# Forget bias of the samples by way of DRAM and VectorE instead of TensorE, with its transfers ahead of the output projection's weights

## What is computed

```
ft   = cumsum(concat(cache_logf[page_table], logf))         # per sample and head, 264 steps
sc   = einsum(q, k_all) * scale
bias = ft[:, :, past:, None] - ft[:, :, None, :]
p    = softmax(where(mask, sc + bias, -inf))                # the ft of the query drops out
y    = einsum(p, v_all)
```

## Time and profile before

| | us |
|---|---|
| median of 3 runs (1370.23 to 1373.33) | 1373.27 |
| the profiled execution | 1372.02 |
| its span, first to last instruction | 1370.3 |
| TensorE busy in the span | 1304.2 (95%) |
| VectorE busy | 357.1 (26%) |
| ScalarE busy | 207.7 (15%) |
| mean rate of the DMA queues | 358 GB/s |

### The profile page before, as it was taken

The page is one execution under the profiler, slowest core; times in us unless marked ns, Lnnn a source line. Parts: engine busy times, 40 slices in busy tenths (PEclk is TensorE's granted clock), DMA queues, the critical chain, the costliest instruction groups (busy, mean ns, idle before and its releaser), DMA issues.

```text
span 1370.3 us, 15525 instructions
## 1 busy us (share of the span) xinstructions
PE 1304.2 (95%) x6186; PEld 580.5 (42%) x6186; DVE 357.1 (26%) x754; ACT 207.7 (15%) x475; POOL 38.4 (3%) x79
## 2 busy tenths in 40 slices
PE   5999999999999999999999999999999999999896
PEld 2656466655463433434344342334334343343332
DVE  2542225766452121112122111211211122121122
ACT  2124424411221100101011010101101010010101
POOL 1100002000020000000000000000000000000000
PEclk9999999999989999999999999999999999999998
DMA  9836586789676999999999999999999999999993
GB/s 345 285 141 266 185 281 173 208 230 260 233 281 242 414 428 428 428 428 427 427 426 428 428 427 428 401 426 425 428 428 429 428 422 429 428 427 428 427 427 137
DMA packets 71905, 491.06 MB, mean 358 GB/s; under 512 B 11814, under 2 KB 24862, under 8 KB 44053
## 3 DMA queue, kind: packets, MB, share of 16 engines
q1 hardware_dynamic: 68564, 480.86, 86.9%
q0 software_dynamic: 3264, 9.13, 2.5%
HBM read 484.77 MB, written 5.18 MB: 358 GB/s over the span
## 4 chain that ended last, share of the span: by engine, by line
PE 65%; DMA 30%; DVE 2%; issue 1%; SPq 1%; ACT 0%; DVEq 0%
PE bank L1949 29%; DMA ring<-in_w_gate_up_dram 27%; PE bank L1632 8%; PE bank L1658 4%; PE bank L1937 3%; PE bank L2016 2%; PE bank L1620 2%; PE bank L1506 2%; PE bank L1787 2%; PE bank L1913 2%; DMA ring<-in_w_in_dram 1%; PE bank L1572 1%; PE bank L1914 1%; PE bank L2044 1%; PE bank L1940 1%
## 5 line engine op out<-in xcount | busy, mean ns | idle before, releaser
L1949 PE MATMUL bank<-ring,work 128*64 128x512 f32 x1984 | 439.9, 597 | 11.2 <-issue 5.9
L1949 PEld LDWEIGHTS bank<-ring,work 128*64 128x64 f32 x1984 | 155.2, 137 | 281.7 <-issue 281.7
L1949 PE MATMUL bank<-ring,hT 128*64 128x512 f32 x896 | 206.2, 608 | 14.1 <-DMA ring<-in_w_gate_up_dram 14.1
L1449 DVE TENSOR_TENSOR gbT<-gbT,bank 128x512 f32<-128x512 f32 x80 | 55.0, 688 | 436.6 <-PE bank L1940 301.6
L1949 PEld LDWEIGHTS bank<-ring,hT 128*64 128x64 f32 x896 | 69.1, 139 | 148.6 <-issue 148.6
L1632 PE MATMUL bank<-hT,ring 128*128 128x320 f32 x384 | 106.8, 439 | 2.1 <-DMA ring<-in_w_in_dram 2.1
L1405 DVE TENSOR_SCALAR work<-bank 128x512 f32<-128x512 f32 x32 | 22.0, 687 | 317.9 <-PE bank L1949 299.1
L1632 PEld LDWEIGHTS bank<-hT,ring 128*128 128x128 f32 x384 | 73.3, 192 | 36.3 <-issue 5.9
L1658 PE MATMUL bank<-hT,ring 128*128 128x320 f32 x256 | 73.6, 437 | 0.2 <-ACT gaT L705 0.2
L1937 PE MATMUL bank<-work 128*128 128x512 f32 x128 | 67.8, 631 | 0.0
L842 ACT ACTIVATE work<-bank 128x320 f32<-128x320 f32 x15 | 6.6, 438 | 394.0 <-PE bank L1506 394.0
(11 more groups left out here) (375 smaller groups left out, 913.0 us busy)
## 6 DMA issues: line engine op xcount, KB each, us to landing
ring<-in_w_gate_up_dram SPq DMA_DIRECT2D x128, 2048.0 KB, 16.0
ring<-in_w_down_dram SPq DMA_DIRECT2D x64, 2048.0 KB, 17.3
ring<-in_w_ada_dram SPq DMA_DIRECT2D x12, 2048.0 KB, 10.6
ring<-in_w_in_dram SPq DMA_DIRECT2D x12, 2048.0 KB, 11.0
ring<-in_cache_k_dram SPq DMA_DIRECT2D x64, 128.0 KB, 6.6
ring<-in_cache_v_dram SPq DMA_DIRECT2D x16, 512.0 KB, 6.4
ring<-in_w_out_dram SPq DMA_DIRECT2D x2, 2048.0 KB, 12.7
out_dram<-tok POOLq DMA_DIRECT2D x2, 1024.0 KB, 8.5
```

Of the source, the lines that this page charges most:

```text
L1449: TTo(piece(gbf, i), piece(gbf, i), B[6 + n % 2][:, :], ALU.add).then_inc(s["scatter_read"], 1)
L1949: last = mm(bank[CAP * x:CAP * x + CAP, :], lhsT[:, CAP * x:CAP * x + CAP], rhs(x), start=start, stop=stop)
```

## The change

The bias leaves TensorE. `cached_logf` becomes two full transposes and one small matmul, for which the cached pages are stored in another order and the new log forget values are spread by sample (`lfnew`). VectorE makes `Fs`, now one row for each sample and head, at the start of prompt pair 7, ahead of `keys_turned(0)`. SP then writes it to DRAM with 16 DMAs, waits until they have landed, and reads it back with 9 DMAs that repeat each row for the 8 queries: the bias of sample b lies in `qT[:, b, 0:256]` (the prompt's queries are done with by then), that of the new columns in `Ftail`. These stand ahead of `chunk(23)`. `sample_max(b)` adds the bias where it copied before, `sscores(b)` has two matmuls fewer.

```diff
+        sbias_d = nc.dram_tensor("sample_bias", (DB, 4, 4, PAST), f32, kind="Internal").ap()
+        stail_d = nc.dram_tensor("sample_tail", (4, 4, DB, DS), f32, kind="Internal").ap()
...
             values_in(0)
             values_in(1)
+            eng.wait_ge(s["F_made"], 2)
+            for b in range(DB):
+                rows = Fs[H * b:H * b + H, :]
+                eng.dma_start(sbias_d[b].rearrange("u g n -> g u n"), rows[:, 0:PAST]).then_inc(s["bias_out"], 16)
+                eng.dma_start(stail_d[:, :, b, :].rearrange("u g q -> g u q"), rows[:, PAST:PAST + DS]).then_inc(s["bias_out"], 16)
+            eng.wait_ge(s["bias_out"], 16 + 32 * DB)
+            eng.wait_ge(s["scores_ps"], H)
+            for b in range(DB):
+                eng.dma_start(qT[:, b, 0:PAST], sbias_d[b].rearrange("u g n -> (u g) n").unsqueeze(1).to_broadcast([H, DS, PAST])).then_inc(s["bias_in"], 16)
+            eng.dma_start(Ftail, stail_d.rearrange("u g b q -> (u g) (b q)").unsqueeze(1).to_broadcast([H, DS, NS])).then_inc(s["bias_in"], 16)
             chunk(23)
             chunk(25)
             keys_in(2)
...
-                V_.tensor_copy(P[:, 0:PAST], ps[:, 0:PAST]).then_inc(s["sscores_read"], 1)
+                if b == 0:
+                    eng.wait_ge(s["bias_in"], 96 + 16 + 16 * DB)
+                TTo(P[:, 0:PAST], ps[:, 0:PAST], qT[:, b, 0:PAST], ALU.add).then_inc(s["sscores_read"], 1)
...
+                new = P[:, PAST + DS * b:PAST + DS * b + DS]
+                link(TTo(new, new, Ftail[:, DS * b:DS * b + DS], ALU.add))
...
                 if p == NT - 1:
+                    eng.wait_ge(s["tr_ps"], G_CF + 1)
+                    link.later(TS(Fs[:, 0:PAST], B[1][:, 0:PAST], -1.0, None, ALU.mult))
+                    link(TS(Fs[:, PAST:PAST + DS], B[0][:, 0:DS], -1.0, None, ALU.mult))
+                    link(V_.tensor_copy(r1, ones[:, 0:2]))
+                    V_.tensor_tensor_scan(Fs, onesf, Fs, 0.0, ALU.mult, ALU.add).then_inc(s["F_made"], 1)
...
-            eng.wait_ge(s["tr_ps"], G_CF + 1)
-            link.later(V_.tensor_copy(Fs[:, :, 0:PAST], B[1][:, :].rearrange("p (s c) -> p s c", s=2)))
...
-            for n in range(2):
-                link(V_.tensor_tensor_scan(Fs[:, n, :], onesf, Fs[:, n, :], 0.0, ALU.mult, ALU.add))
-            TS(Fs, Fs, -1.0, None, ALU.mult).then_inc(s["F_made"], 1)
...
-                for g in range(4):
-                    q = 32 * g
-                    for n in range(2):
-                        for i in range(NPG):
...
+                eng.wait_ge(s["sample_consts"], 1)
+                for i in range(NPG):
+                    tr(B[1][:, 128 * i:128 * i + 128], lfc[:, DB * i:DB * i + DB, :].rearrange("p b h -> p (b h)"), 128)
+                mm(B[0][:, 0:DS], lfnew, at_token, start=True, stop=True).then_inc(s["tr_ps"], 1)
...
-                mm(ps[:, 0:PAST], hsel[q:q + H, :], Fs[q:q + H, n, 0:PAST], start=False, stop=False)
-                mm(ps[:, PAST + DS * b:PAST + DS * b + DS], hsel[q:q + H, :], Fs[q:q + H, n, PAST:PAST + DS], start=False, stop=True)\
-                    .then_inc(s["sscores_ps"], 1)
...
             values(NT - 1)
-            eng.wait_ge(s["F_made"], 2)
```

More of the change, by code:

```diff
@@ L933, in _ @@
             link(V_.reduce_sum(hm4, groups.rearrange("p g h q -> p h g q"), AX.XY))
+            own = ident[0:NS, 0:NS].rearrange("p (b q) -> p b q", q=DS)
+            link.later(V_.reduce_sum(in_sample, own, AX.X))
+            link(V_.reduce_sum(at_token, own.rearrange("p b q -> p q b"), AX.X))
             eng.wait_ge(s["rows_ps"], 1)
@@ L1171, in _ @@
                     head_max(2 * p + 5)
-            eng.wait_ge(s["tr_ps"], G_CF + 1)
-            link.later(V_.tensor_copy(Fs[:, :, 0:PAST], B[1][:, :].rearrange("p (s c) -> p s c", s=2)))
-            for g in range(4):
-                q = 32 * g
-                ins = V_.tensor_copy(Fs[q:q + 32, :, PAST:PAST + DS], B[0][q:q + 32, 0:NS].rearrange("p (s c) -> p s c", s=2)[:, :, DS * g:DS * g + DS])
-                link.later(ins)
-            link(V_.tensor_copy(r1, ones[:, 0:2]))
-            for n in range(2):
-                link(V_.tensor_tensor_scan(Fs[:, n, :], onesf, Fs[:, n, :], 0.0, ALU.mult, ALU.add))
-            TS(Fs, Fs, -1.0, None, ALU.mult).then_inc(s["F_made"], 1)
             queries(0)
@@ L1699, in cached_logf @@
                 eng.wait_ge(s["scores_read"], H - 2)
-                for g in range(4):
-                    q = 32 * g
-                    for n in range(2):
-                        for i in range(NPG):
-                            page_ = NPG * (4 * n + g) + i
-                            mm(B[1][q:q + 32, PAST * n + 128 * i:PAST * n + 128 * i + 128], lfcf[:, H * page_:H * page_ + 32], ident[:, :],
-                               start=True, stop=True)
-                    last = mm(B[0][q:q + 32, 0:NS], lftf[0:NS, 2 * H:2 * H + 32], ident[0:NS, 0:NS], start=True, stop=True)
-                last.then_inc(s["tr_ps"], 1)
+                eng.wait_ge(s["sample_consts"], 1)
+                for i in range(NPG):
+                    tr(B[1][:, 128 * i:128 * i + 128], lfc[:, DB * i:DB * i + DB, :].rearrange("p b h -> p (b h)"), 128)
+                mm(B[0][:, 0:DS], lfnew, at_token, start=True, stop=True).then_inc(s["tr_ps"], 1)
             scores(0)
@@ L1737, in sscores @@
                         t = 2 * g + odd
-                        mm(ps[32 * g:32 * g + 32, 0:PAST + NS], Qbd[:, b % 2, t, :], KT[:, b % 2, t, :],
-                           start=(odd == 0), stop=False)
-                mm(ps[:, 0:PAST], hsel[q:q + H, :], Fs[q:q + H, n, 0:PAST], start=False, stop=False)
-                mm(ps[:, PAST + DS * b:PAST + DS * b + DS], hsel[q:q + H, :], Fs[q:q + H, n, PAST:PAST + DS], start=False, stop=True)\
-                    .then_inc(s["sscores_ps"], 1)
+                        last = mm(ps[32 * g:32 * g + 32, 0:PAST + NS], Qbd[:, b % 2, t, :], KT[:, b % 2, t, :],
+                                  start=(odd == 0), stop=(odd == 1))
+                last.then_inc(s["sscores_ps"], 1)
             def sweights(b):
```

29 lines of the change are left out of this document (14 added, 15 removed).

## The result

| | before | changed |
|---|---|---|
| median, us | 1373.27 (1369.76 to 1373.73, 5 runs) | 1380.06 (1377.83 to 1382.48, 5 runs) |
| profiled execution, us | 1372.02 | 1382.41 |
| its span, us | 1370.3 | 1380.7 |
| last `svalues`, us from the start | 373.83 | 387.15 |
| TensorE busy, us | 1304.2 | 1297.6 |

The ratio is 1.0059, with a 95% interval of 1.0044 to 1.0075. The same kernel, timed a second time beside the experiments, gave 1.0061 (1.0044 to 1.0078). The forecast was 1377.5 in a range of 1370.5 to 1384.0.

What follows compares the result with a forecast made beforehand. The DMA queue, through the landing of sample 2's keys, was taken to set the samples' start: 8.0 us later keys, 0.2 chain, less 4.5 on TensorE, plus 1.5 clock, +5.2 on 1372.3 gives 1377.5 us, range 1370.5 to 1384.

Steps and rivals of the forecast that it cites:

- The bound and the mechanism: Ahead of `svalues(0)`: sample 2's keys land 8.0 us later, outweighing 4.5 us saved on TensorE in six samples.
- The write trip: On SP: `Fs` ready at 272.1, 16 writes 6.7 us, landing 2.3 us, first read at 281.1.
- the mark of 285: Start of SP's reads: before 278 or after 285 would correct the price of the writes.
- From the first read to the keys: DMA queue to sample 2's keys: 16.7 us as before, plus bias 3.3, plus `chunk(23)` 5.5, less 0.5 overlap.
- The overlap with GpSimd's read: GpSimd's prompt read falls partly ahead of the bias, easing the keys' path by 0.5 us; 3.4 at most.
- The chunk's own landing: `chunk(23)` lands at about 295, `gate_job("gb", 4)` ends near 300, ahead of `svalues(0)`: no cost of its own.
- The clock: TensorE's idle time ahead of `svalues(0)` lowers its clock: 1.5 us taken, between nothing and 2.5 us.
- one sign: Profile after: from `svalues(0)` to the first `w_gate_up` DMA, 4.5 us less than before.
- The sum: Whole kernel: 8.0 keys, 0.2 longer chain, less 4.5 TensorE, plus 1.5 clock: +5.2 us on 1372.3.
- (C): Not slower, transfers hidden: 1362 to 1368; decided by sample 2's keys landing less than 4.3 us later; chance 0.05 plus 0.02.
- (A): Sample 2's keys are late by more than what is saved: +4 to +11, 1376 to 1383; chance 0.57.
- (D): Slow trip: 0.6 us a write, 5.2 for landing, bias at the cached keys' rate: 1383 to 1389; chance 0.06.

Runs made afterwards that it cites:

- the fillers: Changed kernel with 14, then 8, independent matmuls in TensorE's wait ahead of `svalues(0)`: 1379.94 us (ratio 1.0053) and 1381.48 us (1.0078).
- both moves: Changed kernel with `chunk(23)` issued ahead of the DRAM trip and two writes instead of sixteen: 1367.99 us, ratio 0.9975.
- all three steps: Changed kernel with `chunk(23)` first, two writes, six bias reads behind sample 2's keys, GpSimd's prompt read behind sample 3's scores: 1368.80 us, ratio 0.9981.

## Why the prediction came out right

**The bound and the mechanism** held; of the sizes, several were off, and that the total lies in the range is in part luck (below). What sets the samples' start is the landing of sample 2's keys, as read from the wait of 4.60 us in the earlier trace rows, and it is more than TensorE's saving. From their landing to `svalues(0)` it is 4.8 us (4.6 forecast). The six later sample scores are 0.75 us shorter each, and no new wait of note stands in samples 1 to 7. The landing itself was forecast 8.0 us late and came 12.9 us late.

**The write trip** was sized too low. `Fs` was ready at 271.3 (272.1 forecast). But a write took 0.65 us (10.4 us for 16) and not 0.42. The size in bytes doesn't set it: the 32-byte rows took as long as the 1 KB rows, and the plain write of 128 rows of 1 KB, with eight times the bytes, 0.33. And the landing took 4.9 us and not 2.3. The prediction took the 2.3 because "it is the same queue"; what counted was what another queue was doing, GpSimd's read, which had been seen, but was given only 0.5 us and to the other side. The first read went out 5.5 us later than forecast (286.6, not 281.1), just past the mark of 285 which the prediction had set for that.

**From the first read to the keys**: forecast 25.0 us, measured 24.4, but by terms that were off against each other. The bias took the 6.4 us that SyncE needs to issue 9 reads and the chunk behind them, not 3.3 by bytes (each read lands 2.5 us after its issue, and the DMA share from 286.6 to 292.4 us is 0.49, so bytes were not the limit). The overlap with GpSimd's read gave 3.4 us, the bound, and not 0.5 (16.7 us from `chunk(25)` to the keys before, 13.3 with the gate chunk ahead of the trip). The chunk was 4.7 to 5.3 us in place of 5.5. The chunk's own landing cost nothing, as said: TensorE waited 2.73 us for it inside a longer wait, though it came at 300.75 and not at about 295, and `gate_job("gb", 4)` ended at 307 and not near 300.

**The clock** cost 4.7 us in one profile and 2.1 in the other, where 1.5 was taken and 2.5 was the bound. It is why one sign failed: from `svalues(0)` to the first `w_gate_up` DMA there should be 4.5 us less than before, and it is 62.97 us against 62.74.

**The sum.** In the profile `svalues(7)` is 13.3 us late where the terms gave 8.0 + 0.2 - 4.5 + 1.5 = 5.2. Measured, they are 12.9 for the landing, 0.2 for the chain behind it, -4.5 for TensorE and 4.7 for the clock. So the prediction was saved in part by what it didn't count, and that is luck. 2.9 of the 13.3 us come back behind the samples: the low clock at the router doesn't occur in the profile after, its 16 matmuls taking 1.97 us (from the last `svalues` to the first expert 38.9 us against 40.6), and the experts take 954.7 us against 955.9. And the profiled execution was 2.4 us above the median, that of before 1.3 below. What is left is 6.8 us between the medians, against +5.2 from a base set 1 us lower. Whether the router's clock is low differs from profile to profile without regard to the change, as said at the fillers. From the last `svalues` to the end the profiles of these kernels range from 991 to 997 us; what sets this spread was not tried.

**A slip without weight.** Against (C) the prediction says that 7.6 MB in 17 us is more than the 380 GB/s that the queue reaches; the earlier trace rows shows 414. The 7.6 MB would need 447, so the argument holds.

**The rivals.** (A), forecast with 0.57, came true as 1376 to 1383, with 1380.06. Of (D), its 0.6 us a write and its landing of 5.2 came nearly true (0.65 and 4.9), but not its price, since the bias didn't run at the keys' rate and GpSimd's read was out of the way. (C), not slower, is what the kernel becomes once the landing is no more than 4.3 us late, as the prediction put its turning point: with both moves the keys land 28.7 us behind the start of the prompt's last softmax product (268.68 to 297.38), against 28.0 before (270.11 to 298.14), so 0.7 us later, and the kernel is 0.25% faster.

## What to carry to other kernels

When results go through DRAM inside a queue that also prefetches, count the issues of each write and read, and look for what stands behind them: a prefetch that doesn't need the trip belongs ahead of its wait. Make the layout on the chip so that the trip takes two DMAs and not sixteen. Look at what the other queues move while the trip waits for its landing. And moving one landing forward helps only until the next one is late: here the first two moves were worth 12.7 us at the keys, and up to 7.7 us more at the same place changed nothing in the time that could be measured, since the cached values then came late.

## What the runs showed of the hardware

The time a small write needs to be confirmed depends on other queues: 1.1 to 1.2 us from the end of its issue with idle DMA engines, 4.3 to 5.0 us in five profiles in which a read of 1.3 MB on GpSimd's queue filled them. For 3.4 us of that read nothing of SyncE's queue started. The Trainium skill, DMA: Bandwidth & Descriptors, section Queues, rings and completion order, says that each engine takes turns between its queues and drains a whole packet of typically 9 to 17 descriptors before it switches. The larger part of the read, `x_prompt`, is 256 rows of 4 KB, 16 for each of the 16 engines if they are spread evenly (an estimate), which is one such packet; so a wait for most of the read doesn't speak against the rule. The trace records single rows; how they were grouped for the engines no run here shows.

A DMA issue on SyncE took 0.58 us with a gap of 0.04 for most of the writes of 16 permuted rows, of 32 bytes and of 1 KB alike, about the same for a repeating read of 128 KB (5.07 us for 8) and for a 2 MB chunk right behind them; 0.33 us for a plain write of 128 rows of 1 KB, 0.73 for the one of 128 rows of 32 bytes behind it. The shape isn't all: the same 2 MB chunk took 0.39 to 0.43 us where it was issued by itself.

The low clock after a wait cost the same program 2.1 us in one execution and 4.7 in another, over the first sample. The Trainium skill, TensorE: Matmul & The Clock Gate, section Part 1: The HAM clock gate, has an idle stretch bring the throttled clock back; the windows at 0.50 to 0.53 behind the waits of 6.61 and 8.84 us agree, and with a wait of only 1.15 us ahead of `svalues(0)`, in the kernel with all three steps, the first sample took the full-clock 8.14 us.
